# One scan of a two-block model: engine orders shifted by one piece, matmuls of two neighbouring heads issued in turn

## The chip, the cores and the metric

The kernel runs on one core of a Trainium2 chip. The metric is the device time of the whole program in microseconds (us), lower is better. Five engines run their own instruction streams and meet only at semaphores: TensorE (PE in the rows; its weight loads are PEld), VectorE (DVE), ScalarE (ACT), GpSimd (POOL) and SyncE (SP), which here only starts transfers.

## The reference, cut to what matters

The program computes two transformer-like blocks over 512 tokens. The change sits in the first block's state-space scan, which is run forwards and backwards over 16 heads, in chunks of 128 tokens:

```python
def ssd_scan(x, dt, a_head, b_mat, c_mat, h0):
    ...
    a_cum = jnp.cumsum(a, axis=-1)
    l_intra = jnp.exp(segsum(a))
    y_diag = jnp.einsum('bclgn,bcsgn,bgrcls,bcsgrp->bclgrp', cc, bc, l_intra, xdt)
    ...
    y_off = jnp.einsum('bclgn,bcgrpn,bgrcl->bclgrp', cc, prev_states, jnp.exp(a_cum))
    y = (y_diag + y_off).reshape(bsz, seqlen, g, r, p)
```

`ssd_bidir` calls it for both directions and adds the two results. The stage that the change touches (`prod_*` in the kernel) computes `y_diag + y_off` of both directions for all heads, when the states are already there.

## The kernel before, in words

Each engine has one method per stage (`prod_t` TensorE, `prod_a` ScalarE, `prod_v` VectorE, `prod_g` GpSimd), and a program runs the stages one after the other on each engine. There is no scheduler: the order written in these methods is the order on the engine, and `wait_ge` on a named signal is all that ties engines together. Ahead of `prod` come the states, behind it the gate stage (`gate_*`, whose TensorE work is the z projection, lines 258 to 260).

The work is cut into 32 pieces, n = 2h + d, for head h (16) and direction d (2). A piece goes through this chain:

- TensorE, line 1089: one 32-row matmul that broadcasts the head's cumulative sums into a whole bank of the matmul memory ("sums n"); four banks take turns, so sums n waits until piece n-4 has left its bank ("decay n-4", "decay min n-4").
- ScalarE, line 1125: exp of that bank into slot n % 4 of SBUF ("decay n").
- VectorE, line 1162, four instructions: the sums less the row's own sum, at most 0, into the other half of slot n % 4 ("decay min n").
- ScalarE, line 1127: exp of that, in place ("decay exp n").
- GpSimd, line 1197: the first half of the slot times C ("queries n").
- The second half of the slot times the masked C B matrix ("weights n"): on GpSimd, line 1201, for d = 0, on VectorE, line 1167, for d = 1.
- TensorE, lines 1110 and 1111, `products_t(h)`: with both pieces of head h ready, 16 matmuls of 128 rows, 64 columns and 128 moving columns. They add up in one half of a bank: head h writes partitions 0 to 63 when h is even and 64 to 127 when h is odd, so the 16 matmuls of one call all use the same half of the array's columns. A matmul in fp32 is two records in the trace.
- VectorE, line 1186, once in two heads: `y_v` takes the finished bank.

Slot n % 4 is free again when `products(n // 2 - 2)` is done; ScalarE's decay n and VectorE's decay min n both wait for that. Every fourth head TensorE computes the next group's C B matrix (line 1075) and VectorE masks it (line 1151). The order on TensorE is: sums of head h, products of head h-1, sums of head h+1, products of head h. On ScalarE it is decay n, decay exp n, decay n+1, decay exp n+1.

Of the kernel before, what the change touches and what calls it, by code (L numbers as in the profile page):

```python
# [8 lines left out]
ALU = mybir.AluOpType  # L9
ACT = mybir.ActivationFunctionType  # L10
# [95 lines left out]
class Program:  # L106
# [951 lines left out]
    def prod_t(self, t):  # L1058
        S, L, PS = self.S, self.L1, self.PS
        for o in range(8):  # L1060
            g = o // 2
            if o == 0:
                t.wait_ge(*S.at("modrow", 6))
                t.wait_ge(*S.at("modset", 4))
                self.modtr_t(t, 6, 4)
                self.modmm_t(t, 7, 6)
            if o == 1:
                self.modtr_t(t, 7, 6)
            if o % 2 == 0:
                if g:  # L1070
                    t.wait_ge(*S.at("cbm", g - 1))
                else:
                    t.wait_ge(*S.at("state", 9))
                for c in range(4):
                    m = t.matmul(PS[2][:, 128 * c:128 * c + 128], self.v(L.CHB + 768 * g + 128 * c, 128), self.v(L.CHC + 512 * g + 128 * c, 128), start=True, stop=True)
                m.then_inc(*S.on("t", "cb", g))
            for h in (2 * o, 2 * o + 1):
                for d in range(2):
                    n = 2 * h + d
                    if n == 0:  # L1080
                        t.wait_ge(*S.at("sum rows"))
                    if n in (1, 2):
                        t.wait_ge(*S.at("modset", (6, 5)[n - 1]))
                    if n >= 4:
                        t.wait_ge(*S.at("decay", n - 4))
                        t.wait_ge(*S.at("decay min", n - 4))
                    rows = slice(32 * (n % 4), 32 * (n % 4) + 32)
                    one = self.cst("ident", 32 * (n % 4) + 16 * d + h, 1)[rows, :].to_broadcast([32, 128])
                    t.matmul(PS[self.SUMS[n % 4]][:, :], one, self.v(L.ACT, 512)[rows, :], start=True, stop=True).then_inc(*S.on("t", "sums", n))
                if h:  # L1090
                    self.products_t(t, h - 1)
        self.products_t(t, 15)

    def products_t(self, t, h):
        S, L, PS = self.S, self.L1, self.PS
        o, hh = h // 2, h % 2
        if hh == 0 and o >= 2:
            t.wait_ge(*S.at("y", o - 2))
        if h == 0:
            for c in range(4):  # L1100
                t.wait_ge(*S.at("xdf", c))
                t.wait_ge(*S.at("xd", c))
        for d in range(2):
            t.wait_ge(*S.at("queries", 2 * h + d))
            t.wait_ge(*S.at("weights", 2 * h + d))
        for c in range(4):
            out = PS[o % 2][64 * hh:64 * hh + 64, 128 * c:128 * c + 128]
            for d in range(2):
                i = (2 * h + d) % 4
                t.matmul(out, self.v((L.XDF, L.XTOK)[d] + 1024 * c + 64 * h, 64), self.v(L.WK + 2048 + 512 * i + 128 * c, 128), start=d == 0, stop=False)  # L1110
                m = t.matmul(out, self.v(self.state(d, c) + 64 * h, 64), self.v(L.WK + 512 * i + 128 * c, 128), start=False, stop=d == 1)
        m.then_inc(*S.on("t", "products", h))

    def prod_a(self, a):
        S, L, PS = self.S, self.L1, self.PS
        self.after(a, "a", "states")
        self.weights_a(a, 32)
        a.activation(self.stat(4)[:, 0:1], self.cst("one1"), ACT.Exp).then_inc(*S.on("a"))
        for o in range(8):
            for n in range(4 * o, 4 * o + 4):  # L1120
                ea, dm = self.v(L.WK + 512 * (n % 4), 512), self.v(L.WK + 2048 + 512 * (n % 4), 512)
                a.wait_ge(*S.at("sums", n))
                if n >= 4:
                    a.wait_ge(*S.at("products", n // 2 - 2))
                a.activation(ea, PS[self.SUMS[n % 4]][:, :], ACT.Exp).then_inc(*S.on("a", "decay", n))
                a.wait_ge(*S.at("decay min", n))
                a.activation(dm, dm, ACT.Exp).then_inc(*S.on("a", "decay exp", n))
        a.wait_ge(*S.at("cb", 3))
        for k in range(8):
            a.wait_ge(*S.at("xn back", k))  # L1130
            if k == 6:
                a.wait_ge(*S.at("queries", 31))
            self.part_hi(a, self.v(L.XR[k], 512), L.XN2 + 512 * k, 512, "xn hi", k)

    def prod_v(self, v):
        S, L, PS = self.S, self.L1, self.PS
        self.after(v, "v", "states")
        self.weights_v(v, 32)
        self.modset_v(v, 6, 4)
        for o in range(8):  # L1140
            g = o // 2
            if o == 1:
                self.modset_v(v, 7, 6)
            if o % 2 == 0:
                v.wait_ge(*S.at("cb", g))
                if g >= 2:
                    v.wait_ge(*S.at("weights", 8 * (g - 2) + 6))
                    v.wait_ge(*S.at("weights", 8 * (g - 2) + 7))
                for d in range(2):
                    cb = self.v(L.WKB + 1024 * (g % 2) + 512 * d, 512).rearrange("p (c t) -> p c t", c=4)  # L1150
                    v.tensor_tensor(cb, PS[2][:, :].rearrange("p (c t) -> p c t", c=4),
                                    self.cst(("triF", "triB")[d]).unsqueeze(1).to_broadcast([128, 4, 128]), ALU.mult).then_inc(*S.on("v", "cbm d", g, d))
                S.mark("v", "cbm", g)
            for h in (2 * o, 2 * o + 1):
                for d in range(2):
                    n = 2 * h + d
                    dm = L.WK + 2048 + 512 * (n % 4)
                    v.wait_ge(*S.at("decay", n))
                    if n >= 4:
                        v.wait_ge(*S.at("products", h - 2))  # L1160
                    for c in range(4):
                        v.tensor_scalar(self.v(dm + 128 * c, 128), PS[self.SUMS[n % 4]][:, 128 * c:128 * c + 128], self.v(L.AC + 32 * c + 16 * d + h, 1), 0.0,
                                        ALU.subtract, ALU.min).then_inc(*S.on("v"))
                    S.mark("v", "decay min", n)
                    if d:
                        v.wait_ge(*S.at("decay exp", n))
                        v.tensor_tensor(self.v(dm, 512), self.v(dm, 512), self.v(L.WKB + 1024 * (g % 2) + 512, 512), ALU.mult).then_inc(*S.on("v", "weights", n))
                if h == 0:
                    self.modrow_v(v, 7, 6)
                if h and h % 2 == 0:  # L1170
                    self.y_v(v, h // 2 - 1)
        v.wait_ge(*S.at("queries", 31))
        for k in (0, 1):
            self.gate_lo(v, "v", k)
        v.wait_ge(*S.at("products", 15))
        for k in (2, 3):
            self.gate_lo(v, "v", k)
        self.y_v(v, 7)
        for k in (5, 6):
            self.gate_lo(v, "v", k)  # L1180

    def y_v(self, v, o):
        S, L = self.S, self.L1
# [4 lines left out]
    def prod_g(self, g):  # L1188
        S, L = self.S, self.L1
        self.after(g, "g", "states")  # L1190
        self.weights_g(g, 32)
        for o in range(8):
            q = o // 2
            for n in range(4 * o, 4 * o + 4):
                ea, dm = self.v(L.WK + 512 * (n % 4), 512), self.v(L.WK + 2048 + 512 * (n % 4), 512)
                g.wait_ge(*S.at("decay", n))
                g.tensor_tensor(ea, ea, self.v(L.CHC + 512 * q, 512), ALU.mult).then_inc(*S.on("g", "queries", n))
                if n % 2 == 0:
                    g.wait_ge(*S.at("cbm", q))
                    g.wait_ge(*S.at("decay exp", n))  # L1200
                    g.tensor_tensor(dm, dm, self.v(L.WKB + 1024 * (q % 2), 512), ALU.mult).then_inc(*S.on("g", "weights", n))
        g.wait_ge(*S.at("products", 15))
        for k in (4, 7):
            self.gate_lo(g, "g", k)
# [3394 lines left out]
```

## Time and profile before

| | us |
|---|---|
| median of 3 runs | 4468.57 (4462.52 to 4469.36) |
| time of the profiled execution | 4467.58 |
| its span, first to last instruction | 4465.8 |
| TensorE busy | 4259.9 (95%) |
| products of heads 1 to 14, start to start of heads 1 and 15 | 78.2 |
| TensorE busy in these 78.2 | 68.5 |

The profiled execution lies 1.0 us under the median and 1.8 us over its own span. The stage of the change is one of some dozens and takes about 96 us, from the first decay at 280.6 us to the last product at 376.4 us of the span. TensorE's granted clock has two levels, which the views give as 1.00 (2.4 GHz) and 0.50 (1.2 GHz).

### The profile page before, as it was taken

The page shows a single profiled execution, that of the slowest core. Times are in us where ns is not written, and L with a number is a line of the kernel's source. Part 1 is how long each engine was busy: PE and PEld are TensorE (multiplying, and loading weights), DVE is VectorE, ACT ScalarE, POOL GpSimd, SP SyncE. Part 2 cuts the span into 40 slices and gives each one's busy share as a digit, 9 for nine tenths or more (in the row PEclk, how much of TensorE's full clock was granted, in tenths as well). Part 3 has the DMA queues.
Part 4 walks back from the last instruction along what each step waited for, and adds up shares of the span by engine and source line. Part 5 has one row for each costly group of instructions (what it writes and reads, how often), then busy time and mean ns, then how long its engine had stood idle before and what let it go on. Part 6 is the DMA issues. An engine that isn't in the chain of part 4 may idle for free.

```text
span 4465.8 us, 66515 instructions
## 1 busy us (share of the span) xinstructions
PE 4259.9 (95%) x26227; PEld 3709.7 (83%) x26227; DVE 3101.2 (69%) x4740; ACT 1807.3 (40%) x2814; POOL 1552.8 (35%) x1005
## 2 busy tenths in 40 slices
PE   7979999999989999999999999999999999989998
PEld 4856755779989999999989877789889877877997
DVE  4766657559887988788878555488478545555873
ACT  4345411233334554333345345355355333323542
POOL 2044224314887656777721110211111110112121
PEclk8989999999999999999999999899999999999999
DMA  4133521224876779999933222133323332102332
GB/s 180 48 109 116 184 74 51 94 89 147 265 240 208 263 287 394 372 385 388 366 110 105 94 90 67 43 100 100 96 94 105 95 103 78 46 35 67 101 100 75
DMA packets 232190, 665.74 MB, mean 149 GB/s; under 512 B 22519, under 2 KB 88455, under 8 KB 229704
## 3 DMA queue, kind: packets, MB, share of 16 engines
q1 hardware_dynamic: 110528, 389.87, 26.2%
q0 software_dynamic: 38752, 142.90, 8.7%
q10 hardware_dynamic: 82600, 128.71, 8.0%
q8 instruction: 210, 3.44, 0.3%
q14 instruction: 100, 0.82, 0.1%
HBM read 593.24 MB, written 68.16 MB: 148 GB/s over the span
## 4 chain that ended last, share of the span: by engine, by line
PE 75%; DVE 15%; POOL 3%; issue 3%; ACT 3%; DMA 2%; ACTq 0%; DVEq 0%; POOLq 0%; SPq 0%
PE ps L258 14%; PE ps L260 14%; PE ps L259 14%; PE ps L2714 5%; PE ps L2716 5%; PE ps L2715 5%; DVE r L227 2%; PE ps L1598 2%; DVE A L2029 2%; PE ps L3749 1%; PE ps L1677 1%; DVE A L2328 1%; POOL r L227 1%; DVE A L2329 1%; DMA A<-in_w_mod 1%
## 5 line engine op out<-in xcount | busy, mean ns | idle before, releaser
L258 PE MATMUL ps<-r,r 128*128 128x384 f32 (+1 forms) x3944 | 1452.9, 368 | 21.5 <-POOL r L227 11.0
L259 PE MATMUL ps<-r,r 128*128 128x384 f32 (+1 forms) x3944 | 1435.2, 364 | 0.0
L260 PE MATMUL ps<-r,r 128*128 128x384 f32 (+1 forms) x3944 | 1435.0, 364 | 0.0
L227 DVE TENSOR_TENSOR r<-A,r 128x1024 fp32r<-128x1024 f32 x436 | 604.1, 1387 | 717.7 <-ACT r L221 710.4
L221 ACT ACTIVATE r<-A 128x1024 fp32r<-128x1024 f32 x513 | 542.3, 1058 | 1203.0 <-PE ps L260 1012.4
L258 PEld LDWEIGHTS ps<-r,r 128*128 128x128 f32 x3944 | 745.0, 189 | 117.6 <-issue 21.3
L259 PEld LDWEIGHTS ps<-r,r 128*128 128x128 f32 x3944 | 744.6, 189 | 81.7 <-issue 3.6
L260 PEld LDWEIGHTS ps<-r,r 128*128 128x128 f32 x3944 | 744.1, 189 | 81.3
L274 ACT ACTIVATE r<-A 128x512 fp32r<-128x512 f32 (+1 forms) x796 | 474.3, 611 | 498.3 <-DVE A L2402 232.8
L2714 PE MATMUL ps<-r,r 128*128 128x256 f32 x2128 | 601.0, 282 | 3.5 <-DVE A L2878 2.6
L2716 PE MATMUL ps<-r,r 128*128 128x256 f32 x2128 | 600.4, 282 | 0.0
L2715 PE MATMUL ps<-r,r 128*128 128x256 f32 x2128 | 599.8, 282 | 0.0
L277 POOL TENSOR_TENSOR r<-A,r 128x384 fp32r<-128x384 f32 (+2 forms) x243 | 335.2, 1387 | 550.8 <-ACT r L274 411.6
L277 DVE TENSOR_TENSOR r<-A,r 128x512 fp32r<-128x512 f32 x617 | 449.6, 744 | 10.5 <-ACT r L274 6.8
L2714 PEld LDWEIGHTS ps<-r,r 128*128 128x128 f32 x2128 | 403.7, 190 | 5.3 <-DVE A L2878 3.4
L2715 PEld LDWEIGHTS ps<-r,r 128*128 128x128 f32 x2128 | 403.7, 190 | 0.2
L2716 PEld LDWEIGHTS ps<-r,r 128*128 128x128 f32 x2128 | 403.7, 190 | 0.0
L2896 POOL TENSOR_TENSOR A<-A 128x512 f32<-128x512 f32 x72 | 120.8, 1678 | 695.5 <-DVE A L2887 695.5
L227 POOL TENSOR_TENSOR r<-A,r 128x1024 fp32r<-128x1024 f32 x77 | 206.5, 2685 | 156.6 <-ACT r L221 155.8
L2016 POOL DMA_INDIRECT A<-in_u_rows,A x128 | 198.9, 1554 | 57.0 <-DVE A L2029 37.1
L2966 DVE TENSOR_TENSOR A<-A 128x512 f32<-128x512 f32 x304 | 208.5, 686 | 4.0 <-issue 0.9
L2029 DVE SCALAR_TENSOR_TENSOR A<-A 128x1024 f32<-128x1024 f32 x128 | 208.5, 1655 | 2.5 <-DMA A<-in_u_rows,A 2.4
(532 smaller groups left out, 5580.9 us busy)
## 6 DMA issues: line engine op xcount, KB each, us to landing
A<-in_pu SPq DMA_DIRECT2D x128, 512.0 KB
A<-in_pv SPq DMA_DIRECT2D x128, 512.0 KB
A<-in_f1i SPq DMA_DIRECT2D x88, 512.0 KB, 3.5
A<-in_f2i SPq DMA_DIRECT2D x88, 512.0 KB, 3.6
A<-in_w_in SPq DMA_DIRECT2D x48, 512.0 KB
acts<-A ACTq DMA_DIRECT2D x128, 192.0 KB
gates<-A ACTq DMA_DIRECT2D x8, 3072.0 KB, 11.8
A<-gates ACTq DMA_DIRECT2D x32, 768.0 KB
```

Of the source, the lines that this page charges most:

```text
L221: a.activation(self.vr(self.wr0 + 2048 * (u % RW), 1024), self.v(self.st0 + 1024 * (u % RS), 1024), ACT.Copy).then_inc(*self.S.on("a", "hi ...
L227: e.tensor_tensor(self.vr(at + 1024, 1024), self.v(self.st0 + 1024 * (u % RS), 1024), self.vr(at, 1024).bitcast(F32), ALU.subtract).then_i ...
L258: t.matmul(o, hi, xh, start=first and k == k0, stop=False)
L259: t.matmul(o, hi, xl, start=False, stop=False)
L260: m = t.matmul(o, lo, xh, start=False, stop=final and k == K - 1)
L274: a.activation(self.vr(at, n), src, ACT.Copy).then_inc(*self.S.on("a", *key))
L277: e.tensor_tensor(self.vr(lo, n), src, self.vr(at, n).bitcast(F32), ALU.subtract).then_inc(*self.S.on(who, *key))
L2029: v.scalar_tensor_tensor(out=row, in0=row, scalar=1.0, in1=self.v(L.XT, 1024), op0=ALU.mult, op1=ALU.mult, accum_out=self.v(L.DOT + c, 1)) ...
L2714: t.matmul(ps[:, 0:256], hi, xh, start=opens and k == 0, stop=False, skip_group_check=not opens)
L2715: t.matmul(ps[:, 0:256], hi, xl, start=False, stop=False, skip_group_check=not opens)
L2716: m = t.matmul(ps[:, 0:256], lo, xh, start=False, stop=k == 3, skip_group_check=not opens)
L2966: v.tensor_tensor(self.operand(i, p, x), self.v(one, 512), self.v(two, 512), how).then_inc(*S.on("v", "sum", i, p, x))
```

## The change

Three things change, and the instructions stay the same in kind and number, except that a few matmuls carry other start and stop flags:

- The products come in 17 calls instead of 16, `products_t(t, j)` with the pieces 2j-1 and 2j, that is the second piece of head j-1 and the first of head j. The first and the last call have one piece. The two heads lie in different column halves, and the matmuls of the two pieces are issued in turn.
- ScalarE issues decay n+1 ahead of decay exp n; VectorE issues decay min n ahead of the weights of n-1, and GpSimd queries n ahead of the weights of n-1 (`weigh`).
- Slot n % 4 is freed by piece: decay n and decay min n wait for "product n-4", which the call with that piece signals, and no longer for both pieces of a head. `y_v` comes half a head later on VectorE.

```diff
-    def products_t(self, t, h):
+    def products_t(self, t, j):
         S, L, PS = self.S, self.L1, self.PS
-        o, hh = h // 2, h % 2
-        if hh == 0 and o >= 2:
-            t.wait_ge(*S.at("y", o - 2))
...
-        for d in range(2):
-            t.wait_ge(*S.at("queries", 2 * h + d))
-            t.wait_ge(*S.at("weights", 2 * h + d))
+        for n in pair:
+            if n % 4 == 0 and n >= 8:
+                t.wait_ge(*S.at("y", n // 4 - 2))
+            t.wait_ge(*S.at("queries", n))
+            t.wait_ge(*S.at("weights", n))
         for c in range(4):
-            out = PS[o % 2][64 * hh:64 * hh + 64, 128 * c:128 * c + 128]
-            for d in range(2):
-                i = (2 * h + d) % 4
-                t.matmul(out, self.v((L.XDF, L.XTOK)[d] + 1024 * c + 64 * h, 64), self.v(L.WK + 2048 + 512 * i + 128 * c, 128), start=d == 0, stop=False)
-                m = t.matmul(out, self.v(self.state(d, c) + 64 * h, 64), self.v(L.WK + 512 * i + 128 * c, 128), start=False, stop=d == 1)
-        m.then_inc(*S.on("t", "products", h))
+            for part in range(2):
+                for n in pair:
+                    h, d = divmod(n, 2)
+                    out = PS[h // 2 % 2][64 * (h % 2):64 * (h % 2) + 64, 128 * c:128 * c + 128]
...
+                    if c == 3:
+                        m.then_inc(*S.on("t", "product", n))
...
-                if n >= 4:
-                    a.wait_ge(*S.at("products", n // 2 - 2))
-                a.activation(ea, PS[self.SUMS[n % 4]][:, :], ACT.Exp).then_inc(*S.on("a", "decay", n))
-                a.wait_ge(*S.at("decay min", n))
-                a.activation(dm, dm, ACT.Exp).then_inc(*S.on("a", "decay exp", n))
...
+                    a.wait_ge(*S.at("product", n - 4))
+                a.activation(self.v(L.WK + 512 * (n % 4), 512), PS[self.SUMS[n % 4]][:, :], ACT.Exp).then_inc(*S.on("a", "decay", n))
+            if n:
+                self.decay_a(a, n - 1)
...
-                    if d:
-                        v.wait_ge(*S.at("decay exp", n))
-                        v.tensor_tensor(self.v(dm, 512), self.v(dm, 512), self.v(L.WKB + 1024 * (g % 2) + 512, 512), ALU.mult).then_inc(*S.on("v", "weights", n))
+                    if n:
+                        self.weigh(v, "v", n - 1)
...
-                if n % 2 == 0:
-                    g.wait_ge(*S.at("cbm", q))
-                    g.wait_ge(*S.at("decay exp", n))
-                    g.tensor_tensor(dm, dm, self.v(L.WKB + 1024 * (q % 2), 512), ALU.mult).then_inc(*S.on("g", "weights", n))
+                if n:
+                    self.weigh(g, "g", n - 1)
```

On GpSimd at the start of the stage, before the change, line 1197 is queries and line 1201 weights (pieces 0 to 7):

```order
L1197 TENSOR_TENSOR A<-A 128x512 [waits s_a,s_v,s_t]
L1201 TENSOR_TENSOR A<-A 128x512 [waits s_a,s_v]
L1197 TENSOR_TENSOR A<-A 128x512 [waits s_a] x2
L1201 TENSOR_TENSOR A<-A 128x512 [waits s_a,s_v]
L1197 TENSOR_TENSOR A<-A 128x512 [waits s_a] x2
L1201 TENSOR_TENSOR A<-A 128x512 [waits s_a,s_v]
```

and after it, where line 1219 is queries and line 1202 weights:

```order
L1219 TENSOR_TENSOR A<-A 128x512 [waits s_a,s_v,s_t]
L1219 TENSOR_TENSOR A<-A 128x512 [waits s_a]
L1202 TENSOR_TENSOR A<-A 128x512 [waits s_a,s_v]
L1219 TENSOR_TENSOR A<-A 128x512 [waits s_a] x2
L1202 TENSOR_TENSOR A<-A 128x512 [waits s_a,s_v]
```

The weights of piece 2j+2 now stand behind the queries of piece 2j+3 in GpSimd's order, where they stood ahead of them.

On TensorE after the third pair of sums, the difference for one call, where lines 1110 and 1111 are the products of one head and lines 1113 and 1115 those of two pieces:

```order
-L1110 MATMUL ps<-A 64x128 [waits s_g,s_v]
-L1111 MATMUL ps<-A 64x128
-L1110 MATMUL ps<-A 64x128
-L1111 MATMUL ps<-A 64x128
...
+L1113 MATMUL ps<-A 64x128 [waits s_g,s_v]
+L1113 MATMUL ps<-A 64x128
+L1115 MATMUL ps<-A 64x128 x2
+L1113 MATMUL ps<-A 64x128 x2
+L1115 MATMUL ps<-A 64x128 x2
```

Two matmuls of one line now follow each other, and they are of different heads, one in each column half.

## Rows read from the trace of the kernel before

**Rows 1.** The page: busy time of each engine, share of the span, instructions.

```profile
PE 4259.9 (95%) x26227; PEld 3709.7 (83%) x26227; DVE 3101.2 (69%) x4740; ACT 1807.3 (40%) x2814; POOL 1552.8 (35%) x1005
```

**Rows 2.** Two stretches: length, busy times PE, PEld, DVE, ACT, POOL, clock, DMA share, GB/s.

```profile
286.60:291.20 4.60, 4.50 (x21) 4.53 (x22) 2.72 (x10) 1.75 (x3) 3.28 (x3) 0.50 0.01 2
294.50:372.70 78.20, 68.51 (x526) 55.31 (x524) 51.09 (x140) 33.50 (x59) 53.19 (x42) 1.00 0.08 28
```

**Rows 3.** Groups of instructions between 293 and 376.3 us.

```profile
L1197 POOL TENSOR_TENSOR A<-A 128x512 f32<-128x512 f32 x28 | 36.0, 1287 | 14.9 <-ACT A L1125 14.9
...
L1201 POOL TENSOR_TENSOR A<-A 128x512 f32<-128x512 f32 x14 | 17.8, 1269 | 12.5 <-ACT A L1127 10.8 <-ACT A L1125 1.7
```

**Rows 4.** The chain, 312.4 to 322.9 us: start, us, what.

```profile
312.41 0.40 PE ps L1110 x2
...
315.87 0.22 PE ps L1111 x2
316.09 1.11 PE ps L1089 x4
317.20 0.59 ACT A L1125
...
319.50 0.59 ACT A L1125
...
320.12 1.14 DVE A L1162 x4
...
321.28 0.64 ACT A L1127
...
321.94 0.85 DVE A L1167
322.80 0.14 issue
322.93 0.29 PE ps L1110
```

**Rows 5.** GpSimd in order of time, 309.1 to 312.5 us.

```profile
309.22 1.27 POOL L1201 TENSOR_TENSOR A<-A 128x512 f32<-128x512 f32 x1 [1.00 <-ACT A L1127]
310.44 1.28 POOL L1197 TENSOR_TENSOR A<-A 128x512 f32<-128x512 f32 x1
311.95 1.44 POOL L1197 TENSOR_TENSOR A<-A 128x512 f32<-128x512 f32 x1 [0.23 <-ACT A L1125]
```

**Rows 6.** In order of time: the start of the stage and its last products.

```profile
280.54 2.08 PE L1089 MATMUL ps<-A 32*128 32x512 f32 x6 [5.27 <-DVE A L615]
...
280.57 0.58 ACT L1125 ACTIVATE A<-ps 128x512 f32<-128x512 f32 x1
...
292.53 1.05 PE L600 MATMUL ps<-A 128*128 128x2 f32 x8
...
294.57 0.32 PE L1110 MATMUL ps<-A 128*64 128x128 f32 x1
...
372.76 0.40 PE L1110 MATMUL ps<-A 128*64 128x128 f32 x2 [1.87 <-DVE A L1167]
...
376.37 0.50 PE L258 MATMUL ps<-r,r 128*128 128x512 f32 x1
```

**Rows 7.** Matmuls of 32 columns in four column quarters: in order of time, and their stretch.

```profile
266.45 3.63 PE L588 MATMUL ps<-A 128*32 128x512 f32 x12
...
266.40:270.10 3.70, 3.63 (x12) 0.56 (x12) 0.50 0.14 27
```

**Rows 8.** Stretches around idle times of TensorE elsewhere, and one in this stage.

```profile
407.30:410.70 3.40, 1.06 (x6) 0.55 (x5) 3.23 (x7) 1.98 (x6) 1.41 (x2) 1.00 0.71 220
410.80:414.10 3.30, 3.30 (x5) 1.24 (x5) 3.23 (x3) 2.40 (x5) 3.30 (x2) 0.50 0.16 59
622.40:629.10 6.70, 5.44 (x6) 2.00 (x7) 6.63 (x12) 0.00 (x0) 4.79 (x4) 0.50 0.00 0
369.80:373.20 3.40, 1.53 (x14) 1.32 (x13) 2.56 (x7) 2.21 (x5) 2.26 (x2) 1.00 0.00 0
```

More of the change, by code:

```diff
@@ L1092, in prod_t @@
         self.products_t(t, 15)
-    def products_t(self, t, h):
+        self.products_t(t, 16)
+    def products_t(self, t, j):
         S, L, PS = self.S, self.L1, self.PS
-        o, hh = h // 2, h % 2
-        if hh == 0 and o >= 2:
-            t.wait_ge(*S.at("y", o - 2))
-        if h == 0:
+        pair = [n for n in (2 * j - 1, 2 * j) if 0 <= n < 32]
+        if j == 0:
             for c in range(4):
@@ L1102, in products_t @@
                 t.wait_ge(*S.at("xd", c))
-        for d in range(2):
-            t.wait_ge(*S.at("queries", 2 * h + d))
-            t.wait_ge(*S.at("weights", 2 * h + d))
-        for c in range(4):
-            out = PS[o % 2][64 * hh:64 * hh + 64, 128 * c:128 * c + 128]
-            for d in range(2):
-                i = (2 * h + d) % 4
-                t.matmul(out, self.v((L.XDF, L.XTOK)[d] + 1024 * c + 64 * h, 64), self.v(L.WK + 2048 + 512 * i + 128 * c, 128), start=d == 0, stop=False)
-                m = t.matmul(out, self.v(self.state(d, c) + 64 * h, 64), self.v(L.WK + 512 * i + 128 * c, 128), start=False, stop=d == 1)
-        m.then_inc(*S.on("t", "products", h))
+        for n in pair:
[3 more added lines that the diff above has]
+            t.wait_ge(*S.at("weights", n))
+        for c in range(4):
+            for part in range(2):
+                for n in pair:
+                    h, d = divmod(n, 2)
+                    out = PS[h // 2 % 2][64 * (h % 2):64 * (h % 2) + 64, 128 * c:128 * c + 128]
+                    if part == 0:
+                        t.matmul(out, self.v((L.XDF, L.XTOK)[d] + 1024 * c + 64 * h, 64), self.v(L.WK + 2048 + 512 * (n % 4) + 128 * c, 128), start=d == 0 and c == 0, stop=False)
+                        continue
+                    m = t.matmul(out, self.v(self.state(d, c) + 64 * h, 64), self.v(L.WK + 512 * (n % 4) + 128 * c, 128), start=False, stop=d == 1 and c == 3)
+                    if c == 3:
+                        m.then_inc(*S.on("t", "product", n))
+                        if d:
+                            S.mark("t", "products", h)
     def prod_a(self, a):
@@ L1118, in prod_a @@
         a.activation(self.stat(4)[:, 0:1], self.cst("one1"), ACT.Exp).then_inc(*S.on("a"))
-        for o in range(8):
-            for n in range(4 * o, 4 * o + 4):
-                ea, dm = self.v(L.WK + 512 * (n % 4), 512), self.v(L.WK + 2048 + 512 * (n % 4), 512)
+        for n in range(33):
+            if n < 32:
                 a.wait_ge(*S.at("sums", n))
                 if n >= 4:
-                    a.wait_ge(*S.at("products", n // 2 - 2))
-                a.activation(ea, PS[self.SUMS[n % 4]][:, :], ACT.Exp).then_inc(*S.on("a", "decay", n))
-                a.wait_ge(*S.at("decay min", n))
-                a.activation(dm, dm, ACT.Exp).then_inc(*S.on("a", "decay exp", n))
+                    a.wait_ge(*S.at("product", n - 4))
+                a.activation(self.v(L.WK + 512 * (n % 4), 512), PS[self.SUMS[n % 4]][:, :], ACT.Exp).then_inc(*S.on("a", "decay", n))
+            if n:
+                self.decay_a(a, n - 1)
         a.wait_ge(*S.at("cb", 3))
@@ L1133, in prod_a, with decay_a @@
             self.part_hi(a, self.v(L.XR[k], 512), L.XN2 + 512 * k, 512, "xn hi", k)
+    def decay_a(self, a, n):
+        S, L = self.S, self.L1
+        a.wait_ge(*S.at("decay min", n))
+        dm = self.v(L.WK + 2048 + 512 * (n % 4), 512)
+        a.activation(dm, dm, ACT.Exp).then_inc(*S.on("a", "decay exp", n))
     def prod_v(self, v):
@@ L1159, in prod_v @@
                     if n >= 4:
-                        v.wait_ge(*S.at("products", h - 2))
+                        v.wait_ge(*S.at("product", n - 4))
                     for c in range(4):
@@ L1164, in prod_v @@
                     S.mark("v", "decay min", n)
-                    if d:
-                        v.wait_ge(*S.at("decay exp", n))
-                        v.tensor_tensor(self.v(dm, 512), self.v(dm, 512), self.v(L.WKB + 1024 * (g % 2) + 512, 512), ALU.mult).then_inc(*S.on("v", "weights", n))
+                    if n:
+                        self.weigh(v, "v", n - 1)
                 if h == 0:
                     self.modrow_v(v, 7, 6)
-                if h and h % 2 == 0:
-                    self.y_v(v, h // 2 - 1)
+                if h >= 3 and h % 2:
+                    self.y_v(v, (h - 3) // 2)
+        self.weigh(v, "v", 31)
         v.wait_ge(*S.at("queries", 31))
@@ L1180, in prod_v, with weigh @@
             self.gate_lo(v, "v", k)
+    def weigh(self, e, who, n):
+        S, L = self.S, self.L1
+        if who != ("v" if n % 2 else "g"):
+            return
+        g, d = n // 8, n % 2
+        dm = self.v(L.WK + 2048 + 512 * (n % 4), 512)
+        e.wait_ge(*S.at("cbm", g))
+        e.wait_ge(*S.at("decay exp", n))
+        e.tensor_tensor(dm, dm, self.v(L.WKB + 1024 * (g % 2) + 512 * d, 512), ALU.mult).then_inc(*S.on(who, "weights", n))
     def y_v(self, v, o):
```

## The prediction

> **What bounds the kernel now.** I read the page first. TensorE is busy for 95% of the 4465.8 us of the span [rows 1], so a stage can give time back only where TensorE waits or works slower than it could. Then the two stretches of this stage. The products of heads 1 to 14 take 78.2 us, 5.59 us a head, at clock 1.00 [rows 2]. TensorE is busy for 68.5 us of them, VectorE for 51.1, GpSimd for 53.2, so none is full. It is a loop through engines that sets the pace.
>
> The chain shows this loop [rows 4]. From one product call to the call two heads later it takes 10.52 us. The 16 matmuls of a head take 3.68 us: 0.22 for each pair of records, one matmul (0.218 over the 15 that follow the first), and 0.19 more at the ends. The sums queued behind them take 1.11. Then ScalarE and VectorE play ping-pong for both pieces: decay 0.61, decay min 1.17, decay exp 0.53, decay 0.62, decay min 1.16, decay exp 0.66, each timed start to start. The weights of the second piece and the hand-over to TensorE take 0.99. Where the C B matrix comes in, it is longer, which makes the mean of 5.59 out of 5.26. The change takes the ping-pong apart, so what matters is the next loop.
>
> **What the column halves give.** All 16 matmuls of a call use one half of the columns today. After the change neighbours use different halves. The nearest row is line 588, with 128 rows and 32 columns in four column quarters: 12 records of 1.06 us each, six matmuls, stand in 3.63 us, at clock 0.50 [rows 7]. One after the other, at 0.218 us for 128 columns at 1.00, six of 512 columns would need 6 x 4 x 0.218 x 2 = 10.5 us. So matmuls that differ in column quarter alone do run together, each with its own weights and its own moving data. I take the halves as together: a call of 16 matmuls takes 8 x 0.218 = 1.74 us, and 1.93 with the 0.19. The bounds are this and, without any overlap, 3.49 and 3.68.
>
> The Trainium skill, "TensorE: Matmul & The Clock Gate", section on packing small matmuls, says that a weight load overlaps matmuls in flight only when the row group differs; here both pieces use all rows. By it the sum would lie between the two bounds, near the upper one, and the forecast would become the slower rival below. Rows 7 speak against it: the loads of line 588 use all rows too.
>
> **The next loop.** The slot of decay n is free when product n-4 is done, so decay 2j+3 on ScalarE waits for call j, which holds piece 2j-1. GpSimd's order then has queries 2j+3 ahead of weights 2j+2, and weights 2j+2 are what call j+1 needs. So from the start of call j to the start of call j+1:
>
> - call j and its hand-over: 1.93 us
> - decay 2j+3, start to start as in the chain: 0.62 [rows 4]
> - queries 2j+3 on GpSimd: 1.22 start to start where nothing keeps it [rows 5]; its mean duration is 1.29 [rows 3]
> - weights 2j+2 on GpSimd: 1.27 [rows 3], and 0.14 of issue to TensorE as in the chain [rows 4]
>
> That is 5.18 us a head, against 5.59. Everything else fits under it. TensorE has 1.93 + 1.11, VectorE 51.1 / 14 = 3.65, GpSimd 53.2 / 14 = 3.80. The decay exp of 2j+2 on ScalarE is issued behind decay 2j+3 and takes 0.66, but GpSimd is still at queries 2j+3. The sums wait for nothing: they follow the call and end 2 us before the next. The masking of the C B matrix and `y_v`, which comes half a head later, lie in VectorE's spare 1.5 us; the bank that `y_v` empties is wanted two heads on. No transfer and no weight preparation changes its place, and the edits of the start and stop flags cost nothing, as the matmuls stay the same. With this the loop gives 14 x 0.41 = 5.7 us.
>
> **Start and end.** The first decay at 280.57 us stays [rows 6]. Now queries 0, queries 1 and weights 0 follow; piece 1's decay waits for its sums, a row of 2.08 us from 280.54 [rows 6], so until about 282.7; queries 1 start 0.6 later, and with 1.22 and 1.27 behind each other weights 0 end near 285.9 and call 0, eight matmuls at clock 0.50, is over by 289.5 (8 x 0.436). The small matmuls and the third pair of sums behind it take 2.0 us, as from 292.53 to 294.57 [rows 6], and with the hand-over and the low clock I put the start of call 1 near 291.9, against 294.57 for head 1. From there 14 loops of 5.18 take 72.5 us, call 15 starts at 364.4, call 16, a single piece, follows 1.84 behind (its weights are done by VectorE about when call 15 starts), and its last result is there 1.86 later, at 368.1. The z projection starts 3.61 us behind the start of head 15's call today, at 376.37 [rows 6]. **With the clock at 1.00 throughout the change gives about 8.2 us.**
>
> **What the clock takes.** Calls of half the length leave TensorE idle. In a loop of 5.18 us it works 1.74 + 0.19 + 1.11, some 3.0 us, and is then idle for about 2.1 to 2.2. Elsewhere such gaps cost the clock: 1.06 us busy in 3.40, and the 3.30 us behind it are at 0.50 [rows 8]. In this stage a stretch with 1.53 busy in 3.40 still kept 1.00 [rows 8], with an idle 1.87 in it [rows 6], and the 78.2 us ran at 1.00 with 12% idle [rows 2]. The new gap is longer than that and comes in every loop. A call at 0.50 takes 1.74 us more, and it is on the loop: 6.92 us. In such a loop TensorE works 5.6 us and idles for 1.3, which is what the clock comes back in: a low stretch of 6.70 us elsewhere had 5.44 busy [rows 8]. So I expect the clock to fall and return several times. A low stretch there lasts 3.3 to 6.7 us, one loop, and I take one in three of the 16 calls, 5 to 6, as slow: 5.5 x 1.74 = 9.6 us. The sum is then -8.2 + 9.6 = +1.4 us. The bounds are no slow call (-8.2) and all 16 (+19.6); break-even is at 4.7 slow calls.
>
> **Behind the stage.** The z projection needs the same parts on ScalarE, VectorE and GpSimd, which are released by the same last product, so a shift of the stage passes on as it is. The page gives no transfer queue that would be waited for here: the DMA share is 0.08 [rows 2].
>
> **Sum.** The profiled execution took 4467.58 us, so 4469.0 for this one; the median of the three runs is 1.0 us above that execution, which makes 4470.0.
>
> **Rivals.**
>
> - *The clock holds.* For it: 369.8 to 373.2 us kept 1.00 with 1.87 idle [rows 8]. Against it: the gap is 0.3 longer and comes 14 times. It gives -8.2, 4460.4. It passes 0.2% (8.9 us) only if one of the terms is also a bit better, as 5.1 for 5.18 in the loop.
> - *The halves don't overlap*, so the change doesn't do what it says: calls take 3.68 us and the same loop through GpSimd is 6.93 us. For it: only the skill's sentence. Against it: rows 7. Call 1 at 291.9, 14 loops of 6.93, then 3.6 + 1.9: 394.4, 18 us later than today, 4486.6. It decides from a call of about 2.5 us on: 14 x 0.54 = 7.6 on top of +1.4 passes 8.9.
> - *The clock is low for most of the stage.* 11 slow calls or more: -8.2 + 19.1 = +10.9, 4479.5. For it: once down, a loop still has 1.3 us idle.
> - *GpSimd slows.* It took 1.44 us where VectorE's weights ran beside it, against 1.28 just before [rows 5]. With 0.17 on both operations of each loop, 14 x 0.34 = 4.8 us is added: 4474.8. Alone this does not decide, together with seven slow calls it does.
>
> **How the numbers follow.** A measurement of this kernel can tell about 0.2%, 8.9 us, from no change. Overlap with some slow calls, from 1 to 10, gives -6.5 to +9.2, and I give it 0.67; the clock holding 0.12; the clock mostly low, or slow calls with a slow GpSimd, 0.13; no overlap 0.08. Faster than 4459.7 comes from half of the second case and a little of the first, 0.12. Slower than 4477.5 comes from the last two and the end of the first, 0.2. The range leaves out the no-overlap case and the worst of the low clock below it, and reaches to the holding clock: 4460 to 4479.
>
> **What would show it.** Two records of different heads starting within some 0.01 us of each other, a call's first to last record at 1.7 us; decay 2j+3 on ScalarE idle until TensorE; queries then weights on GpSimd without a gap; TensorE released by GpSimd's line 1202; calls 5.2 us apart at clock 1.00 and 6.9 at 0.50; a granted clock with 0.50 in the stretches of 295 to 365 us. The forecast fails if the clock stays at 1.00, if a call takes over 2.5 us at full clock, or if TensorE waits for another engine than GpSimd.

## The result, and the profile after

The changed kernel takes 4484.38 us (median of 20 runs, 4470.35 to 4498.52) against 4469.94 us for the kernel before (20 runs, 4462.52 to 4484.47). The ratio is 1.0028, with a 95% interval of 1.002 to 1.0037: about 12.5 us slower, and the two medians lie 14.4 us apart. The forecast was 4470, with a range from 4460 to 4479.

The page of the changed kernel, against [rows 1]:

```profile
span 4485.0 us, 66531 instructions
PE 4261.7 (95%) x26227; PEld 3706.1 (83%) x26227; DVE 3104.7 (69%) x4740; ACT 1805.6 (40%) x2814; POOL 1548.8 (35%) x1005
```

Busy time hardly differs; 19 us of span are added. The page hides what happened in the stage: TensorE is busy there for 77.9 us, against 82.0 before, because its lower clock takes back most of what the overlap saves. The profiled executions differ ahead of the stage too, where both kernels hold the same instructions: the first decay stands at 286.07 us here and at 280.57 before, and in the profiles below anywhere from 279.2 to 288.9. So the stage is measured by itself from here on, from the first decay to the first matmul of the z projection. In order of time, TensorE and ScalarE of the changed kernel:

```profile
286.07 0.58 ACT L1131 ACTIVATE A<-ps 128x512 f32<-128x512 f32 x1
...
295.03 1.87 PE L600 MATMUL ps<-A 128*128 128x2 f32 x8
296.83 2.07 PE L1089 MATMUL ps<-A 32*128 32x512 f32 x4
298.84 0.69 PE L1113 MATMUL ps<-A 128*64 128x128 f32 x4
...
388.95 0.70 PE L1113 MATMUL ps<-A 128*64 128x128 f32 x4 [3.39 <-POOL A L1202]
...
394.05 0.50 PE L258 MATMUL ps<-r,r 128*128 128x512 f32 x1
```

The stage takes 394.05 - 286.07 = 108.0 us, against 376.37 - 280.57 = 95.8 [rows 6]. That is +12.2, about the whole of the measured difference. Its parts against the row pairs of before: up to call 1, 12.8 against 14.0 us; from call 1 to call 15, 90.1 against 78.2; from call 15 to the z projection, 5.1 against 3.6.

The chain of the changed kernel shows one slow call and one fast one:

```profile
331.00 0.70 PE ps L1113 x4
331.70 0.43 PE ps L1115 x4
...
334.47 0.60 ACT A L1131
...
335.14 0.49 POOL A L1219
...
336.37 1.28 POOL A L1202
337.64 0.14 issue
337.78 0.44 PE ps L1113 x4
338.22 0.22 PE ps L1115 x4
...
339.77 0.04 issue
339.81 0.60 ACT A L1131
340.41 0.07 issue
340.48 0.49 POOL A L1219
340.97 0.73 issue
341.71 1.27 POOL A L1202
342.98 0.14 issue
343.12 0.44 PE ps L1113 x4
```

The reader sees the loop of the forecast, step by step: the call (1113, 1115), decay on ScalarE (1131), queries (1219) and weights (1202) on GpSimd, the next call. The 0.49 and the 0.73 of issue are one operation, the queries; GpSimd's next record starts before the first has ended. Four records stand in 0.22 us where one matmul's two stood before [rows 4], so the column halves do run together. The fast loop is 5.34 us (337.78 to 343.12), the slow one 6.78. The one difference is the call: 4 records take 0.43 us instead of 0.22, which is the clock of 1.2 GHz. Of the calls 1 to 15 only three, 3, 7 and 11, run wholly at 2.4 GHz; the other twelve are slow for the whole of their length or a part.

Stretches of the changed kernel, in the columns of [rows 2]:

```profile
300.00:365.00 65.00, 48.59 (x408) 36.06 (x404) 39.01 (x105) 22.41 (x41) 39.95 (x31) 0.74 0.07 26
320.00:340.00 20.00, 14.09 (x131) 10.86 (x130) 12.00 (x31) 6.89 (x13) 11.61 (x9) 0.82 0.00 1
340.00:360.00 20.00, 14.99 (x109) 10.14 (x106) 10.61 (x28) 6.58 (x13) 11.60 (x9) 0.60 0.00 1
```

A mean clock of 0.74 in 65 us, of levels 0.50 and 1.00, means that it was low for about half of the time. The three fast calls are those that follow a C B matrix, the additional matmuls of line 1075 that TensorE gets once in four heads. Ahead of them it idles for 0.64, 1.25 and 0.56 us; ahead of most others, with no such work, for 2.3. Around call 3, which is fast, and call 4, which is slow again:

```profile
308.87 1.71 PE L1075 MATMUL ps<-A 128*128 128x128 f32 x8
...
312.28 0.44 PE L1113 MATMUL ps<-A 128*64 128x128 f32 x4 [0.64 <-POOL A L1202]
...
317.62 0.70 PE L1113 MATMUL ps<-A 128*64 128x128 f32 x4 [2.32 <-POOL A L1202]
```

Who waited for whom, 298 to 388 us (total, times, longest):

```profile
ACT A L1131 <- PE ps L1115: 49.0, 14, 4.4
DVE A L1174 <- ACT A L1131: 39.0, 18, 3.7
POOL A L1219 <- ACT A L1131: 38.5, 17, 4.2
PEld ps L1113 <- POOL A L1202: 35.4, 13, 3.1
```

ScalarE's decays wait for the call, GpSimd for the decays, TensorE for GpSimd's weights: TensorE, ScalarE and GpSimd stand in one ring.

### The profile page after: what moved, and what is told of

Its sections match the earlier page's. It is cut to its first block, busy times and chain, and to the rows that moved or that the text cites. A ratio compares the mean times of both kernels' runs of the same rounds, so it can differ in the third digit from the quotient of the medians.

```text
span 4485.0 us, 66531 instructions
## 1 busy us (share of the span) xinstructions
PE 4261.7 (95%) x26227; PEld 3706.1 (83%) x26227; DVE 3104.7 (69%) x4740; ACT 1805.6 (40%) x2814; POOL 1548.8 (35%) x1005
## 4 chain that ended last, share of the span: by engine, by line
PE 75%; DVE 14%; POOL 4%; ACT 3%; issue 3%; DMA 2%; ACTq 0%; DVEq 0%; POOLq 0%; SPq 0%
PE ps L258 14%; PE ps L259 14%; PE ps L260 14%; PE ps L2734 5%; PE ps L2736 5%; PE ps L2735 5%; DVE r L227 2%; PE ps L1618 2%; DVE A L2049 2%; PE ps L3769 1%; PE ps L1697 1%; DVE A L2348 1%; POOL r L227 1%; DVE A L2349 1%; DMA A<-in_w_late 1%
```

## The experiments

Each was run beside the kernel before on the same chip, and the ratio is to that: e1 to e4 beside 4468.75 us (28 runs), e5 to e8 beside 4471.15 (20), e9 to e12 beside 4469.69 (18). "Stage" is from each run's profile, as is the mean distance of calls 1 to 14 and the clock between 300 and 365 us. In e3 and e10 the last 6 us of that stretch belong to the z projection. A stage is that of one execution, which need not be the median one: the profile of e12 is of its second slowest run (4480.57 us), that of e7 of its fastest (4457.99).

| run | time, us (runs) | ratio to before, 95% | stage, us | calls apart, us | clock |
|---|---|---|---|---|---|
| before | 4469.94 (20) | | 95.8 | 5.59 | 1.00 |
| changed | 4484.38 (20) | 1.0028 (1.002 to 1.0037) | 108.0 | 6.41 | 0.74 |
| e4 changed, again | 4481.78 (10) | 1.0021 (1.0011 to 1.0031) | 110.4 | 6.50 | 0.74 |
| e1 changed, 6 spare matmuls | 4467.47 (12) | 0.9992 (0.9982 to 1.0003) | 93.9 | 5.55 | 1.00 |
| e12 changed, 2 spare matmuls | 4475.13 (10) | 1.0007 (0.9997 to 1.0017) | 103.6 | 6.04 | 0.84 |
| e2 pieces in sequence | 4468.33 (10) | 1.0002 (0.9993 to 1.0011) | 92.4 | 5.36 | 1.00 |
| e8 in sequence, freed by head | 4498.61 (4) | 1.0071 (1.0057 to 1.0086) | 121.6 | 7.58 | 0.87 |
| e3 even weights ahead | 4447.02 (5) | 0.9942 (0.9929 to 0.9955) | 79.3 | 4.60 | 0.92 |
| e9 the same, again | 4453.67 (6) | 0.9963 (0.9949 to 0.9977) | 79.9 | 4.52 | 0.92 |
| e6 e3 with 2 spare matmuls | 4452.34 (6) | 0.9958 (0.9945 to 0.9972) | 78.8 | 4.44 | 0.95 |
| e7 GpSimd's order alone | 4464.61 (10) | 0.9991 (0.9982 to 1.0) | 89.7 | 5.07 | 0.92 |
| e5 e3 in sequence | 4458.67 (7) | 0.9968 (0.9957 to 0.9979) | 78.0 | 4.57 | 1.00 |
| e10 the same, again | 4453.72 (5) | 0.9964 (0.9951 to 0.9977) | 78.4 | 4.57 | 1.00 |
| e11 before, 3 spare matmuls | 4480.34 (5) | 1.0024 (1.0007 to 1.004) | 98.0 | 5.83 | 1.00 |

### Is it the clock? Spare matmuls (e1, e12, e4, e11)

Ahead of each product call from head 3 on, behind the sums, TensorE gets work that nobody reads:

```diff
+            if h >= 3:
+                self.fill_t(t, 6, h)
             if h:
                 self.products_t(t, h - 1)
...
+        for i in range(k):
+            t.matmul(self.PS[6][:, 0:128], self.cst("ident"), self.v(self.L1.ACT, 128), start=True, stop=True)
```

Expected of the six:

> The changed kernel with six spare 128x128 matmuls on TensorE between the sums and the next product call from head 3 on; their results are read by nobody. Theory A (the calls sit on a loop through ScalarE and GpSimd of 5.3 us; TensorE idles 2.3 us in it and its clock falls to 0.50 for about half the stage): the spare 1.3 us lie inside the idle time, the clock reads 1.00 from the fourth call on, all calls take 1.97 us and stand 5.3 to 5.5 us apart, and the time is about 4464 us, 6 under the kernel before and 20 under the changed kernel. Rival B (the new orders themselves lose the time, the low clock only goes with it): the calls stay 6.4 us apart on average and the time is 4484 us or more.

Of the changed kernel as it is:

> The changed kernel once more, beside the others on the same chip. Theory A: calls 5.3 us apart at clock 1.00 and 6.8 to 7.1 us apart at 0.50, in numbers that differ from run to run, so the time differs between executions by more than that of the kernel before; 4484 us, from 4470 to 4498. Rival B: the calls keep one distance of 6.4 us whatever the clock reads.

Of two instead of six:

> The changed kernel with two spare matmuls, 0.44 us, in each loop in place of six. Theory A: TensorE idles 1.8 us in a loop instead of 2.3, as long as in the kernel before, so most stretches keep the clock at 1.00 and at most a few calls are slow: 4466 to 4474 us. Rival H (only an almost full TensorE keeps the clock): as many slow calls as without, 4482 us.

Of three in the kernel before:

> The kernel before with three spare matmuls, 0.65 us, between the sums and the products of each head from head 3 on. Theory A: the clock of this stage is 1.00 already, so spare work can give nothing; where TensorE still waits for weights it costs nothing, elsewhere up to 0.65 us a head: 4470 to 4478 us. Rival G (spare matmuls help by something else than the clock): the time is under 4465 us.

The six spare matmuls take the time to 4467.5 us, where the changed kernel as it is took 4481.8 on the same chip (4484.4 in its first 20 runs); expected were 4464. Their stretch is at 1.00:

```profile
300.00:365.00 65.00, 57.97 (x602) 44.51 (x602) 45.18 (x120) 26.97 (x49) 47.50 (x36) 1.00 0.03 11
```

From the third call on all calls last 1.97 us, 5.35 to 5.6 us apart. The ring is the same, TensorE only works in the time that it would have waited. Two spare matmuls leave 5 of 14 loops in which the clock falls after the start (behind the calls 5, 6, 9, 10 and 14 the loop takes over 6 us), the stretch is at 0.84, and the time lies between: 4475.1, just over the 4466 to 4474 of theory A and nearer to it than to the 4482 of H. In the kernel before, whose clock is at 1.00 anyway, spare matmuls give nothing: its stage grows by 2.2 us. Its time grew by 10.6 us to 4480.3, over the 4470 to 4478 that were expected, in five runs that spread from 4467.7 to 4488.1; that more than the 2.2 is due to the spare matmuls of this stage is not shown. Rival G falls. With e1 rival B falls too: the orders do not lose the time, the clock does. The changed kernel once more has its fast loops of 5.34 us at the same three calls, 3, 7 and 11, and six of 7.05 us or more against three, with 10 runs from 4471.4 to 4488.6.

### Are matmuls in turn worth anything? (e2, e8)

The loops of `products_t` are turned round, so that the first piece is done before the second begins:

```diff
-        for c in range(4):
-            for part in range(2):
-                for n in pair:
+        for n in pair:
+            for c in range(4):
+                for part in range(2):
```

> The changed kernel with the two pieces of a call one after the other instead of in turn, all else as it is. Theory A: nothing runs together any more, a call takes 3.7 us at clock 1.00, the loop is 5.3 + 1.74 = 7.0 us, 14 loops are 98 us against 78 before, and the time is 4490 to 4500 us. Rival C (matmuls issued in turn gain little, since weights of 128 rows are loaded one after the other): a call takes what it takes in turn and the time is that of the changed kernel, 4484 us.

Both theories missed. The time is that of the kernel before, 4468.3, the stage is 15.6 us shorter than in turn, and calls of 3.30 us stand 5.36 us apart. (The stage is also 3.4 us shorter than that of the kernel before; the time, with an interval of 0.9993 to 1.0011, can't show so little.) Its stretch and its chain show why:

```profile
300.00:365.00 65.00, 55.41 (x456) 43.52 (x456) 44.53 (x121) 27.49 (x50) 45.54 (x37) 1.00 0.04 16
```

```profile
333.15 0.40 PE ps L1113 x2
333.56 0.22 PE ps L1115 x2
...
334.65 0.28 PE ps L1113 x4
334.92 0.17 PE ps L1115 x3
335.10 0.02 issue
...
335.18 0.61 ACT A L1131
335.79 0.07 issue
335.86 0.49 POOL A L1219
336.35 0.73 issue
337.08 1.28 POOL A L1202
338.36 0.14 issue
338.49 0.40 PE ps L1113 x2
```

The call starts at 333.15 and ScalarE's decay at 335.18, 2.03 us later, exactly as in turn (337.78 to 339.81), although the call goes on for another 1.3 us. The decay waits for piece 2j-1 alone, the first of the call. In sequence this piece is finished when half the matmuls are done; in turn both pieces are finished together, at the same moment. Overlap brings the second piece forward, for which nobody in this ring waits. What it does do is to leave TensorE idle, and with that goes the clock. What the freeing by piece is worth is tested by taking it away, in sequence:

```diff
-                    a.wait_ge(*S.at("product", n - 4))
+                    a.wait_ge(*S.at("products", n // 2 - 2))
...
-                        v.wait_ge(*S.at("product", n - 4))
+                        v.wait_ge(*S.at("products", h - 2))
```

> The kernel with the two pieces of a call in sequence, and slots freed by head again: decay n and decay min n wait for both pieces of the head of n-4. Theory A (in sequence the first piece of a call frees its slot half a call early, and that hides the missing overlap): decays of a pair now wait for a later call or for the end of this one, the loop grows by 1.3 to 1.8 us, calls 6.7 to 7.1 us apart, time 4487 to 4495 us. Rival F (the freeing by piece does nothing): 4468 us, as in sequence with the freeing by piece.

The edit does less than its expectation says. Piece 2j-1 is the later one of its head, so decay 2j+3 waits for the same half-call signal as in e2. What changes is decay 2j+2: it was free since call j-1 and now waits for that signal too. GpSimd in such a loop, between calls that start at 324.78 and 331.79:

```profile
327.49 2.93 POOL L1219 TENSOR_TENSOR A<-A 128x512 f32<-128x512 f32 x2 [2.85 <-ACT A L1131]
330.38 1.25 POOL L1202 TENSOR_TENSOR A<-A 128x512 f32<-128x512 f32 x1
```

Two queries now stand on the ring where one stood (2.93 us for 1.23). The calls are 7.01 us apart where the clock is at 1.00, and 7.58 on average, since the longer waits cost this kernel its clock as well. 4498.6 us is 3.6 over the upper end of what theory A gave, and 30 from rival F. So, in sequence at least, the shifted orders need the freeing by piece, because it keeps the even piece off the ring. That the decay starts at half a call is read from the rows of e2; no run takes it away.

### Where is the ring? (e3, e7, e9, e5, e10, e6)

The weights of even pieces go back ahead, on ScalarE (the exp they need) and on GpSimd:

```diff
-            if n:
-                self.decay_a(a, n - 1)
+            if n and n % 2 == 0:
+                self.decay_a(a, n - 1)
+            if n % 2 == 0 and n < 32:
+                self.decay_a(a, n)
...
-                if n:
-                    self.weigh(g, "g", n - 1)
+                self.weigh(g, "g", n)
```

> The changed kernel with the weights path of even pieces put back ahead: ScalarE issues decay exp 2j ahead of decay 2j+1, and GpSimd weights 2j ahead of queries 2j+1. Theory A: weights 2j+2 then hang on call j-1 and no longer on call j, so the loop spans two calls and GpSimd with its three operations (3.8 us) or nearly that sets the pace: calls 4.0 to 4.3 us apart, TensorE idle about 1.1 us in each, clock mostly 1.00, time 4446 to 4453 us. Rival B (the shift by one piece was not the binding place, the freeing by piece or the clock is): calls stay 5.3 us or more apart, time 4463 to 4484 us.

With GpSimd's part of it alone:

> The changed kernel with GpSimd's order alone put back: weights 2j ahead of queries 2j+1; ScalarE stays shifted. Theory A: the queries of 1.22 us leave the loop, but decay exp 2j+2 still stands behind decay 2j+3 on ScalarE, so weights 2j+2 still hang on the call just ended: 1.97 + 0.53 + 0.76 + 1.41 = 4.7 us at clock 1.00, idle 1.6 us, 4460 to 4470 us. Rival E (GpSimd's order is all there is to it): the time of both together, 4447 us.

With both, 4447.0 us, and 4453.7 when run again; calls are mostly 4.1 to 4.3 us apart (4.7 to 4.9 where a C B matrix comes in) when the clock is at 1.00. The chain of the first in such a place, where lines 1221 and 1204 are GpSimd's queries and weights, has left the ring and stays on one engine:

```profile
340.90 1.27 POOL A L1204
342.17 1.98 POOL A L1221 x2
344.15 0.97 issue
345.12 1.26 POOL A L1204
346.38 2.12 POOL A L1221 x2
```

With GpSimd's order alone the fast calls are 4.70 us apart, the sum of 4.7 that was expected, and the time is 4464.6. That is far from the 4447 of rival E, so both orders hold the ring; from the kernel before it can hardly be told (0.9982 to 1.0).

The same in sequence, and with spare matmuls:

> The orders of the last but one run (weights path of even pieces ahead) with the two pieces of a call in sequence, no longer in turn. Theory A (what is left of the loss is the low clock, which matmuls in turn bring on by leaving TensorE idle): the call takes 3.3 to 3.7 us, and with its sums TensorE is busy for nearly 4.9 us, so now TensorE sets the pace: calls 4.9 to 5.0 us apart, clock 1.00, 4461 us; matmuls in turn are worth 14 us here, where they are worth minus 14 in the changed kernel. Rival D (matmuls in turn never pay in this stage): the time is under 4447 us.

> The kernel with the weights path of even pieces ahead and matmuls in turn, with two spare matmuls, 0.44 us, in each loop from head 3 on. Theory A: the clock reads 1.00 from the fourth call on, all calls are 4.2 us apart in place of 4.6 on average, 4442 us. Rival B (the spare work only delays, the clock does not set the calls): 14 x 0.4 us more than without, 4453 us.

> The kernel with the weights path of even pieces ahead and matmuls in turn, again, beside its version in sequence on one chip. Theory A: with both, the stage takes 78 to 80 us, since in sequence TensorE is busy for the 4.3 us between calls and in turn the queues of GpSimd hold 4.2 with a slow call now and then. Both come out 16 to 22 us under the kernel before and within 5 us of each other. Rival D (matmuls in turn are worth some 10 us more once the orders are mended, as 4447 against 4459 suggested): this one is again 8 us or more under the other.

> The same orders with the pieces of a call in sequence, again. Theory A: a stage of 78 us, calls 4.3 us apart at clock 1.00, 4450 to 4455 us. Rival D: 4459 us against 4447 for the one in turn.

In sequence the calls are 4.32 us apart, 5.40 with a C B matrix, and TensorE is full:

```profile
300.00:365.00 65.00, 64.26 (x544) 51.60 (x542) 51.45 (x140) 33.09 (x60) 51.51 (x42) 1.00 0.08 28
```

The expected 4.9 us was wrong. It took the upper one of the two lengths given for the call, 3.7, and the call takes 3.33 us: the last matmuls of the first piece run together with the first of the second (the row of 4 records in 0.28 us above). The sums add 0.99. The time was 4458.7 us for 4461.

Side by side on one chip the two came out at 4453.67 and 4453.72 us, 16.0 under the kernel before each. The 12 us between e3 and e5, which had run on two chips, did not come again; what made them is not shown. So the rival of the second pair, that matmuls in turn are worth some 10 us more, falls, and with it theory A of e5, which gave them 14. The rival of e5 said that they never pay in this stage: its number, under 4447, did not come, but neither pair of stages shows a gain from them. In turn GpSimd sets the pace at 4.2 us, and the clock falls now and then; in sequence TensorE is full at 4.3 and keeps its clock.

Spare matmuls on top of the version in turn did to the clock what was expected: calls last 1.97 us from call 2 on and stand 4.14 to 4.24 us apart, 4.7 with a C B matrix. But that makes 4.44 on average and not 4.2, against 4.60 and 4.52 without, and the stage is hardly shorter, 78.8 us against 79.3 and 79.9. So the expected 4442 us was missed by 10. The 4452.3 measured are near the 4453 of rival B, whose reason does not hold, as no call came later; they are also near the 4453.7 that the same kernel without spare matmuls took in e9.

## Why the prediction was wrong

- **The loop** was right: call, decay, queries, weights, as put on record. It measured 5.34 us at clock 1.00, not 5.18: 2.03 for the call and its hand-over (1.93), 0.67 for the decay (0.62), 1.23 for the queries, 1.41 for the weights. At clock 1.00 the gain would be 3.5 us over 14 loops, not 5.7.
- **The column halves** run together, as read from [rows 7]. In the fast call above the first matmuls of both pieces start 0.01 us apart and the next ones 0.04. The loads of their weights, of 128 rows each, start 0.04 us apart:

```profile
337.75 0.23 PEld L1113 LDWEIGHTS ps<-A 128*64 128x64 f32 x4 [2.05 <-POOL A L1202]
```

The Trainium skill, "TensorE: Matmul & The Clock Gate", section on packing small matmuls, lets a weight load overlap matmuls in flight only when the row group differs. The rows of this case disagree: these four loads use all rows, and the last of them starts (337.84) and ends (337.98) after the first matmul has started (337.78). The measurement decides.
- **Start**: 1.2 us earlier, not 2.7. The small matmuls and the sums behind call 0 ran at the low clock and took 3.8 us (295.03 to 298.84), where 2.0 was taken from a row at 1.00.
- **What the clock takes** is the step that failed, by its size. I took one call in three as slow, 5 to 6 calls, 5.5 x 1.74 = 9.6 us. Twelve of the calls 1 to 15 were slow in whole or in part. Their share of the 14 loops is 90.1 - 14 x 5.34 = 15.3 us, and 1.4 more sit in call 15 (5.1 us to the z projection against 3.7 forecast). That is 16.7 us, as much as 9.6 whole calls. I had read rows in which the clock falls once and returns, and no row in which the same gap comes back every five microseconds. The sum with what was measured: -1.2 - 3.5 + 15.3 + 1.5 = +12.1 us for the stage, against +1.4 forecast. Of these 10.7 us the clock makes 7.1, the loop 2.2 and the start 1.5. With the clock term alone off, the sum would have been +8.5, about 4477 us and still inside the range; the loop and the start did the rest.
- **The rival "the clock is low for most of the stage"** (+10.9, 4479.5, with 11 slow calls), at 0.13 together with a slow GpSimd, comes nearest. It is near in part by luck: the clock was low for about half of the time, and its price of 9.6 whole calls lies inside the case of 1 to 10 slow calls, which had 0.67.
- **The rival "the halves don't overlap"** was worked out wrongly: 6.93 us a loop and 4486.6. Run e2 has no overlap but at the seam and takes 4468.3. I had put the whole call on the ring, when with slots freed by piece only its first piece is on it. By the same error the gain of 8.2 us was made to hang on the overlap. What there is of it belongs to the orders and the freeing by piece: e2 has 3.4 us of stage without overlap (92.4 against 95.8).
- **GpSimd slows** did not show on the ring: 1.23 us for the queries and 1.27 for the weights.

So the cause is shown in three ways. Give TensorE work, and 14 us of the time and 14 to 17 us of the stage are gone (e1). Give it less, and a part of them is: 4475.1 us lies about half way, the stage of 103.6 a third (e12). Don't overlap, and calls 1 to 14 keep the clock; only part of the last ones is slow (e2).

## What to carry to other kernels

When a matmul burst is made shorter but its engine waits on a ring for the next one, the burst's end is worth only what somebody waits for in it, and the idle time behind it can cost the clock for much of what follows: count the idle time per loop before shortening. Signal each piece when it is ready, and let the consumer of the first piece start under the second; this gave in sequence what overlap was to give. In shifted orders look for the one operation that is ready a loop early but stands behind one that isn't: putting even weights ahead of the next queries and decay took 14 us off the stage in sequence (92.4 to 78.0 and 78.4) and 28 in turn (108.0 to 79.3 and 79.9); with spare matmuls in both, which keep the clock up, it was 15 (e1 to e6, 93.9 to 78.8).

## What the runs showed of the hardware

Column halves of 64 with all 128 rows run together in fp32: four records in 0.22 us at 2.4 GHz, twice the rate of one half (two in 0.22). When the half changes between two runs of matmuls, the seam overlaps by itself and a call of 16 takes 3.33 instead of 3.68 us. A TensorE that works about 3.0 of every 5.3 us moved between its two clock levels all through the stage, while 3.3 us of calls and 1.1 of sums in 5.4 (e2) kept 1.00. Whether the time became less even is not shown: 20 runs of the changed kernel lie within 28 us, those of the kernel before within 22, and the ten of e4 within 17.
